# Moving the second block's first inputs into the second gate stage, and five modulation slots to the end of the recurrent mixer

## The reference

```
x = layer_norm(ALPHA * x + 0.5 * swiglu(x, ...), g, b)
y = mixer(x); x = layer_norm(ALPHA * x + y, g, b)
x = layer_norm(ALPHA * x + 0.5 * swiglu(x, ...), g, b)
x = x + sigmoid(x @ ple_wg + ple_bg) * (p @ ple_wp)
```

```
h  = x  * (1 + sc1)  + sh1      # tokens
hc = xc * (1 + csc1) + csh1     # context, from the input
q, k, v = split(h @ w_in), split(hc @ w_in)
```

## Time and profile before

| | |
|---|---|
| median of 3 runs | 2394.52 us (2393.4 to 2398.42) |
| profiled execution | 2394.99 us, its span 2393.7 |
| mean granted TensorE clock | 0.975 of full |
| PE busy | 94% of the span |
| DVE, ACT, POOL busy | 53%, 45%, 2% |
| DMA | 353.6 MB, mean 148 GB/s |

### The profile page before, as it was taken

One profiled execution on the slowest core, in us unless ns is written; L12 is line 12 of the kernel. 1 busy time (PEld: TensorE's weight loads), 2 busy tenths in 40 slices (PEclk: granted clock), 3 DMA queues, 4 the chain that ended last, 5 costly groups with the idle time before them and its releaser, 6 DMA issues.

```text
span 2393.7 us, 39354 instructions
## 1 busy us (share of the span) xinstructions
PE 2254.1 (94%) x17046; PEld 2022.7 (85%) x17046; DVE 1269.7 (53%) x1954; ACT 1077.3 (45%) x1713; POOL 54.3 (2%) x100
## 2 busy tenths in 40 slices
PE   6999989999999999989996989999999999998998
PEld 5999869998999799879995766888888886567997
DVE  3445566556555666365556326764443663455665
ACT  3444455445444554354445526552332451354544
POOL 0000100000000000000000000000000000000000
PEclk9999999999999999989998999999999999999999
DMA  8454525545554544245545121022223433203451
GB/s 315 177 193 176 224 106 218 198 165 218 188 193 168 209 187 165 106 179 195 190 159 194 71 71 53 1 106 89 88 88 119 155 131 129 100 13 138 186 194 54
DMA packets 51628, 353.60 MB, mean 148 GB/s; under 512 B 8064, under 2 KB 8448, under 8 KB 8832
## 3 DMA queue, kind: packets, MB, share of 16 engines
q1 hardware_dynamic: 47520, 346.05, 38.5%
q10 hardware_dynamic: 864, 4.63, 0.5%
q0 software_dynamic: 3072, 0.40, 0.1%
HBM read 349.61 MB, written 1.05 MB: 146 GB/s over the span
## 4 chain that ended last, share of the span: by engine, by line
PE 86%; DVE 7%; ACT 3%; DMA 1%; issue 1%; SPq 0%; POOL 0%; ACTq 0%; DVEq 0%
PE ps L784 13%; PE ps L785 13%; PE ps L786 13%; PE ps L2490 5%; PE ps L920 5%; PE ps L2491 5%; PE ps L2492 5%; PE ps L390 3%; PE ps L391 2%; PE ps L392 2%; PE ps L2220 2%; PE ps L2221 2%; PE ps L2222 2%; PE ps L1455 1%; PE ps L973 1%; PE ps L986 1%
## 5 line engine op out<-in xcount | busy, mean ns | idle before, releaser
L365 DVE TENSOR_TENSOR wl<-ring,wh 128x1024 fp32r<-128x1024 f32 x406 | 477.6, 1221 | 269.1 <-ACT wh L360 268.9
L784 PE MATMUL ps<-xs,wh 128*128 128x256 f32 x1760 | 503.8, 286 | 27.0 <-DVE wl L365 14.1
L785 PE MATMUL ps<-xs,wl 128*128 128x256 f32 x1760 | 502.1, 285 | 0.0
L786 PE MATMUL ps<-xs,wh 128*128 128x256 f32 x1760 | 501.9, 285 | 0.0
L360 ACT ACTIVATE wh<-ring 128x1024 fp32r<-128x1024 f32 x406 | 405.0, 1049 | 167.0 <-PE ps L786 127.1
L784 PEld LDWEIGHTS ps<-xs,wh 128*128 128x128 f32 x1760 | 342.1, 194 | 31.0 <-issue 21.0
L785 PEld LDWEIGHTS ps<-xs,wl 128*128 128x128 f32 x1760 | 342.3, 194 | 0.0
L786 PEld LDWEIGHTS ps<-xs,wh 128*128 128x128 f32 x1760 | 342.1, 194 | 0.0
L784 PE MATMUL ps<-hh,wh 128*128 128x256 f32 x880 | 249.2, 283 | 0.7 <-DVE hl L886 0.7
L785 PE MATMUL ps<-hh,wl 128*128 128x256 f32 x880 | 249.1, 283 | 0.0
L786 PE MATMUL ps<-hl,wh 128*128 128x256 f32 x880 | 249.1, 283 | 0.0
(11 more groups left out here) (441 smaller groups left out, 4016.7 us busy)
## 6 DMA issues: line engine op xcount, KB each, us to landing
ring<-wstream SPq DMA_DIRECT2D x329, 1024.0 KB, 4.9
ada_rows<-ada_stage POOLq DMA_DIRECT2D x96, 4.0 KB, 4.1
CN<-consts ACTq DMA_DIRECT2D x1, 1136.0 KB, 15.7
X<-xin ACTq DMA_DIRECT2D x1, 1024.0 KB, 10.6
X<-cin ACTq DMA_DIRECT2D x1, 1024.0 KB, 9.2
out<-X SPq DMA_DIRECT2D x1, 1024.0 KB, 3.9
PT__65<-pin ACTq DMA_DIRECT2D x1, 512.0 KB, 18.9
ab_w<-wab ACTq DMA_DIRECT2D x1, 512.0 KB, 3.5
```

What stands on the lines that cost most here:

```text
L365: dve.tensor_tensor(lo, tile_of(i), hi.bitcast(F32), ALU.subtract).then_inc(low_part, 1)
L784: pe.matmul(out, wh[:, w, c, :], x_hi, start=start, stop=False, skip_group_check=True)
L785: pe.matmul(out, wl[:, w, c, :], x_hi, start=False, stop=False, skip_group_check=True)
L786: return pe.matmul(out, wh[:, w, c, :], x_lo, start=False, stop=True, skip_group_check=True)
```

## The change

- Five of the modulation slots move from the second gate stage to the end of the recurrent mixer, between the second and the third `c_out` slot in load order; PE multiplies them right after the mean squares. The last z tile moves ahead of the last output products, and all silus come before the norm.
- `pe_adaln` and `dve_adaln` move into the second gate stage, behind its first two tiles. The context is loaded at the end of the recurrent mixer, and `ple_pp` moves to other memory.
- In the second gate stage ACT modulates the context, DVE each finished chunk of x, and both split the results and the first even slot, between the gate tiles. The scaling by ALPHA comes later.
- In the first gate stage the first four weight tiles of `ffn1_1` are split between the gate tiles, and the input's high parts follow chunk by chunk.
- `X` is no longer written ahead of the gate: its sum takes the norm's offset directly.

```
-            + [("ple_g_0", 1), ("ada", 1)] * 4 + [("ada", 1), ("ffn1_1", 33), ("ada", 3), ("c_g", 1)]
+            + [("ple_g_0", 1), ("ada", 1)] * 2 + [("ple_g_0", 2), ("ada", 3), ("ffn1_1", 33), ("ada", 3), ("c_g", 1)]
...
-            + [("c_out", 4), ("ada", 3), ("ffn2_1", 33), ("ple_p_1", 1)] + [("ple_g_1", 1), ("ada", 1)] * 4
-            + [("ada", 1), ("l0_in", 9), ("rpb", 2), ("l0_out", 4), ("l0_ffn", 40),
+            + [("c_out", 2), ("ada", 5), ("c_out", 2), ("ada", 3), ("ffn2_1", 33), ("ple_p_1", 1), ("ple_g_1", 4)]
+            + [("l0_in", 9), ("rpb", 2), ("l0_out", 4), ("l0_ffn", 40),
...  pe_ple
-            pe_ada(8)
+            pe_ada(8) if i == 0 else pe_adaln()
             for t in range(2, 8):
                 pe.wait_ge(*((ple_proj, 4 * i + t + 1) if t < 4 else (ple_gate, 8 * i + t - 3)))
                 pe_tile(t0 + t, PLE_BANK[t % 4])
-                if t % 2:
+                if i == 0 and t in (3, 5):
                     pe_ada(8)
-            pe_ada(8)
+            if i == 0:
+                pe_ada(16)
...  act_ple
-                if t + 4 < 8:
+                if i == 0 or t + 4 < 8:
                     act_high(t0 + t + 4)
+                if i == 0 and t in (3, 5, 6):
+                    act_ada(128 + {3: 8, 5: 16, 6: 24}[t])
+                if i == 1:
+                    if t in (2, 3, 4, 5):
+                        act_context(2 * t - 4)
+                        act_context(2 * t - 3)
+                    if t == 4:
+                        act_slot_high(0)
+                    for q in {5: (0, 1), 6: (2,), 7: (3,)}.get(t, ()):
+                        act_even_high(q)
+            if i == 0:
+                for q in range(4):
+                    c = slice(2 * q, 2 * q + 2)
+                    act.wait_ge(x_ple, 2 * q + 2)
+                    act.activation(xs[:, c, 0, :], X[:, 0, c, :], ACT.Copy).then_inc(x_high, 1)
...  dve_ple
-            dve_x(f"ffn2_{i}")
-            dve.wait_ge(*x_normed(f"ffn2_{i}"))
+            name = f"ffn2_{i}"
+            dve.wait_ge(z_gained, 8 * LNS.index(name) + 8)
+            if i == 1:
+                dve_adaln()
             for t in range(8):
-                if t + 4 < 8:
+                if i == 0 or t + 4 < 8:
                     dve_low(t0 + t + 4)
...
-                dve.scalar_tensor_tensor(X[:, 0, t, :], ple_th[:, t, :], 0.5, X[:, 0, t, :], ALU.mult,
+                dve.scalar_tensor_tensor(X[:, 0, t, :], Z[:, 0, t, :], pcol(LN_GB[name][1], t), ple_th[:, t, :], ALU.add,
                                          ALU.add).then_inc(x_ple, 1)
+                if i == 1:
+                    if t >= 3:
+                        for c in {3: (0, 1), 4: (2, 3), 5: (4, 5), 6: (6,), 7: (7,)}[t]:
+                            dve_modulate(c)
+                    if t == 4:
+                        dve_slot_low(0)
+                    for q in {5: (0,), 6: (1, 2), 7: (3,)}.get(t, ()):
+                        dve_even_low(q)
+            if i == 0:
+                dve_xlow("ffn1_1", X[:, 0])
...  pe_mixer_c
             outputs(2, 2)
+            tile(31)
             outputs(3, 7)
...
             pe.wait_ge(*c_o_a.at("ln1"))
-            pe_ada(8)
+            pe_ada(48)
...  act_mixer_c
             norm_o(2, 0)
             norm_o(3, 1)
-            act_high(t0 + 35)
-            act_ada(320)
-            act.wait_ge(*c_o_v.at("z0"))
+            act_ada(328)
             for k in range(4):
-                if k == 1:
-                    act.activation(c_z[:, 6:8, :], c_z[:, 6:8, :], ACT.Silu).then_inc(*c_o_a("z67"))
                 act.wait_ge(*c_o_v.at(f"z{k}"))
                 act.activation(xs[:, 2 * k:2 * k + 2, 0, :], c_o[:, 2 * k:2 * k + 2, :], ACT.Copy).then_inc(x_high, 1)
+                act_ada(336 + 8 * k)
```

More of the change, by code:

```diff
@@ L180, in _plan @@
     first, last, both = TILE0["c_k"], TILE0["c_out"] + 8, TILE0["l0"]
+    gate = TILE0["ple_g_1"]
     for i in range(len(TILES)):
-        BUF.append((i - first) % 4 if first <= i < last else (i - both) % 4 if both <= i < both + 7 * NPAIR else i % NB)
+        BUF.append((2, 3, 4, 5, 2, 3, 0, 1)[i - gate] if gate <= i < gate + 8 else (i - first) % 4 if first <= i < last else (i - both) % 4 if both <= i < both + 7 * NPAIR else i % NB)
         PREV.append(max((j for j in range(i) if BUF[j] == BUF[i]), default=None))
@@ L197 @@
 LN_COLS = ["l0_1", "l0_2", "l1_1"]
-X_MADE = ["ffn1_0", "ffn2_0", "ffn1_1", "ffn2_1", "l1_2"]
+X_MADE = ["ffn1_0", "ffn1_1", "l1_2"]
 LN_AB = {"ffn2_0": ("ab", 2), "ffn2_1": ("c", 10)}
@@ L829, in act_ffn @@
                 act.wait_ge(gate_up_done, NT * f)
-            if src is not None:
+            else:
                 act_xhigh(src)
@@ L868, in dve_ffn @@
             i0 = TILE0[name]
-            if src is not None:
+            if f == 0:
                 dve_xlow(name, src)
@@ L1306, in dve_add_branch @@
             dve.scalar_tensor_tensor(z, row(t % 4), coef, z, ALU.mult, ALU.add).then_inc(z_done, 1)
-        ple_pp, ple_th = (put(n, [8, T], over=(b, 8192)) for n, b in (("ple_pp", "X"), ("ple_th", "Z")))
+        ple_th = put("ple_th", [8, T], over=("Z", 8192))
+        ple_pp = put("ple_pp", [8, T], over=("free", 512))
         ple_hb = put("ple_hb", [2, 8], over=("free", 0))
@@ L1330, in act_ple_proj @@
                 act.wait_ge(*raw_tile(f"ple_p_{i}", 2 * k + 1))
-                act.activation(flat(ple_pp, k), ps[:, (6, 7, 0, 1)[k], :], ACT.Copy).then_inc(ple_proj, 1)
+                act.activation(flat(ple_pp, k), ps[:, (6, 7, 0, 1)[k], :], ACT.Copy, scale=0.5).then_inc(ple_proj, 1)
         def pe_ple(i):
@@ L1436, in build_program @@
         c_o_p = Steps(sem("c_out_tensor"), [f"o{c}" for c in range(4)] + [f"var{c}" for c in range(4)])
-        c_o_a = Steps(sem("c_out_scalar"), [f"sq{c}" for c in range(4)] + [x for c in range(4) for x in (f"ln{c}", f"rn{c}")]
-                      + ["z67"])
+        c_o_a = Steps(sem("c_out_scalar"), [f"sq{c}" for c in range(4)] + [x for c in range(4) for x in (f"ln{c}", f"rn{c}")])
         c_o_v = Steps(sem("c_out_vector"), [f"r{c}" for c in range(4)] + [f"z{n}" for n in range(4)])
@@ L1860, in z_tile @@
                 act.wait_ge(*tile_done(t0 + 24 + t))
-                act.activation(c_z[:, t, :], row(t % 2), ACT.Silu if t < 6 else ACT.Copy).then_inc(c_z_a, 1)
+                act.activation(c_z[:, t, :], row(t % 2), ACT.Silu).then_inc(c_z_a, 1)
             z_tile(0)
@@ L2360, in square @@
                 act.activation(e_sq[:, u % 2, :], ps[:, E_BANK[u], :], ACT.Square).then_inc(e_sq_a, 1)
[L2361 to L2365, removed]
             act_slot_high(1)
@@ L2379, in act_even_mixer @@
             act_slot_high(4)
+            act.wait_ge(x_ple, 16)
+            act_scale("even", slice(0, 2))
             for t in range(4):
@@ L2413, in dve_even_mixer @@
         def dve_even_mixer():
[L2414 to L2428, removed]
             dve_slot_low(1)
@@ L3006, in act_program @@
             act_layer_norm("ffn2_0", ahead=tiles("ple_g_0"))
-            act_ple(0, "ffn2_0")
-            act.wait_ge(x_ple, 8)
-            act_ffn(2, "ffn1_1", X[:, 0], copies=168)
+            act_ple(0)
+            act_ffn(2, "ffn1_1", X[:, 0], ahead=4, copies=168)
             act_layer_norm("ffn1_1", 192, ahead=tiles("c_k"))
             act_mixer_c()
-            act_layer_norm("c", 344, ahead=tiles("ffn2_1"))
+            act.dma_start(X[:, 1, :, :], cin).then_inc(in_ctx, 16)
+            act_layer_norm("c", 384, ahead=tiles("ffn2_1"))
             act_ffn(3, "ffn2_1", None, ahead=2)
             act_layer_norm("ffn2_1", ahead=tiles("ple_g_1"))
[L3015 to L3018, removed]
+            act_ple(1)
             act_even_mixer()
@@ L3049, in dve_program @@
             dve_ple(0)
-            dve_ffn(2, "ffn1_1", X[:, 0], half)
+            dve_ffn(2, "ffn1_1", X[:, 0], half, ahead=4)
             dve_norm_to_parts("ffn1_1", tiles("c_k"))
```

58 lines of the change are left out of this document (37 added, 21 removed).

## The result

The changed kernel took 2371.06 us (median of 4 runs, 2367.02 to 2374.37) beside 2393.96 us for the kernel before on the same chip: ratio 0.9912, 95% interval 0.9896 to 0.9927, so about 22.9 us faster. The profiled execution took 2374.37 us, at a span of 2373.1. In a second series on another occasion it took 2366.55 us beside 2391.44 (ratio 0.9902, 0.9887 to 0.9917), 24.9 us faster. Forecast were 2368.0 us and 26.5 us of gain.

The account below looks back on a forecast made before the run. TensorE, busy 94% of the span, was taken as the bound, so gains lie in its pauses, double work or low clock. -26.0 - 4.5 + 4.0 = -26.5 from 2394.99 gave 2368.5, forecast 2368 us; range 2361 to 2379.

Parts of the forecast that it names:

- Part C: Second gate stage into the first even tile: tile ends at 1297.4 instead of 1323.4, gain 26.0 us (20 to 28).
- about half a microsecond: Second gate stage: tanh 5 and 6 on ACT run this late, and no gate tile waits for them.
- the longer queue: Second gate stage: DVE's queue outlasts ACT's, its last low part ending at 1295.4 after ACT's last high part.
- hidden work is not hidden: Rival, 16%: second gate stage's modulation and splitting still follow the last gate tile; gain 16.5 instead of 26, 2377.5 us.
- The steps taken to cost nothing: Later ALPHA scaling in the second gate stage costs nothing; context load at the mixer's end costs nothing (0 to 1 us).
- Part B: Recurrent mixer's end: six modulation slots wait for ring loads, `c_out` starts 5.8 us later; cost 4 us (0 to 8).
- the 1.7 forecast: Within `c_out`: the low clock loses 2.4 us instead of 4.1, so 1.7 us of the later start is taken back.
- the tail is cheap: Rival, 14%: at the mixer's end loads land faster or PE's own tail is shorter; cost 0, 2364 us.
- Part A: First gate stage into `ffn1_1`: early weight splits shorten PE's pause and keep the clock up; gain 4.5 us (1 to 7.5).
- perhaps 0.3 later, since ACT first waits for the slot: First gate stage: the last tanh is done at 592.8 or 0.3 later; `ffn1_1` starts at 596.9, 2.7 us less.
- The second term: Start of `ffn1_1`: a pause of 2.7 us leaves the clock alone, saving the 1.8 us lost at half clock before.
- the one row behind the pause at 802.25: Kernel before: a PE pause of 2.67 us left the clock at 1.00, so low clock was not expected after similar pauses.

Follow-up runs that it names:

- two early tiles: Changed kernel, but only two of the four first `ffn1_1` weight tiles are split early in the first gate stage: 2362.21 us, ratio to before 0.9874.
- both edits: Changed kernel with two early `ffn1_1` tiles instead of four and three of the five tail slots inside the mixer's z tiles: 2356.99 us, ratio 0.9859.
- small loads: Changed kernel, but three of the five modulation slots at the mixer's end load only 256 of 2048 columns (output wrong): 2359.05 us, ratio 0.9870.

## Why the prediction was right, and where not

**Part C, the second gate stage, was sized right: 25.9 us measured (25.5 in the second execution), 26.0 forecast.** `pe_adaln` takes 1.42 us (12 matmuls at 1275.54; 1.4 forecast) in the gate stage. The pauses for the second and fourth quarter of the input are 0.73 and 1.84 us ("about 1 and 2"), and the first even tile is done 8.6 us behind the last gate tile (8.5). This is ScalarE's timeline there:

```profile
1292.12 0.46 ACT L1357 ACTIVATE ple_th<-ps,ple_hb 128x256 f32<-128x256 f32 x1
1292.91 1.06 ACT L1426 ACTIVATE e_xh<-H 128x1024 fp32r<-128x1024 f32 x1 [0.33 <-DVE H L1419]
1294.36 0.48 ACT L1357 ACTIVATE ple_th<-ps,ple_hb 128x256 f32<-128x256 f32 x1 [0.39 <-PE ps L393]
1298.92 1.06 ACT L1426 ACTIVATE e_xh<-H 128x1024 fp32r<-128x1024 f32 x1 [4.09 <-DVE H L1419]
...
1303.00 0.60 ACT L2411 ACTIVATE e_sq<-ps 128x512 f32<-128x512 f32 x1 [1.22 <-PE ps L2274]
```

ScalarE stood idle for 0.39 us ahead of the last tanh, waiting for its tile, so the added work fits; the two tanh before it had no idle time ahead of them, 0.3 and 0.7 us late by the step of 2.87 us ("about half a microsecond"). The last high part waits 4.09 us for the vector engine, which was named as the longer queue. The clock was 1.00 there, as forecast. That is not certain, though: in the second execution it fell behind the 1.82 us pause, at a cost of about 2 us (last section); in the five other executions with these splits between the tiles it stayed at 1.00. The runs bear the mechanism out: put the splits behind the tiles, and 9.0 us come back; the rival "hidden work is not hidden" had priced that at 9.5. The steps taken to cost nothing cost nothing: the rest of the kernel is 1070.1 us for 1070.2 of before, and the early context load landed 4.7 us after its issue at 1042.87 (9.2 in before) with nothing waiting for it.

**Part B, the mixer's tail, was right in mechanism: 4.0 forecast, 5.0 in the first execution, 4.2 by the means of all.** Slots 3 to 5 were to land at 1020.7, 1023.3 and 1025.9; they were taken at 1020.61, 1024.84 and 1027.25, and `c_out` started at 1029.11 instead of 1027.8. The later start is partly given back, since the clock comes back sooner within `c_out`: 7.1 us late at the start, 4.78 late at `ffn2_1` (1064.88 for 1060.10), so 2.3 for the 1.7 forecast. The rival "the tail is cheap" fell: no execution with all its slots and full loads had a tail of before's length (the shortest was 47.0).

**Part A, the first gate stage, was wrong in size: 4.5 forecast, 0.4 to 0.6 measured.** The step that failed is "perhaps 0.3 later, since ACT first waits for the slot". ScalarE waited for three loads (3.90, 1.04 and 1.97 us), the last tanh came 1.7 us later than in before, and the input's high parts, which stand behind the last early cast in its order, came with it. The product began at 598.74 and not at 596.9. The second term went with the first: the pause was 3.37 us and not 2.7, and the clock fell to 0.50 as in before, so the 1.8 us of clock were not gained. That term had a weak premise besides: it took the one row behind the pause at 802.25 as what such a pause does, and in eight of the ten traces the clock fell to half behind that very pause (last section). The run with two early tiles shows that the idea was sound and its amount too large: 5.9 us in the stage, more than the 4.5 forecast.

**The sum.** By stages it is -25.9 + 4.2 - 0.6 = -22.3, measured 22.9 and 24.9, forecast 26.5. Between forecast and stages the miss is the first part's 3.9 us; the rest agrees within half a microsecond. The timed medians test this less sharply: the same kernel's two lie 4.5 us apart (2371.06 and 2366.55), so that the total came within 3.1 us of the forecast says little by itself. Two slips in the recorded working are small: the half clock ahead of 603.5 lasts 3.9 us from 599.61 and not 3.7, and 1.07 x 2 is 2.1, not 1.9 (the slots took 1.94).

## What to carry to other kernels

Work that is moved ahead into an in-order queue brings its waits along: before an engine with slack is given a weight split early, look when the load that it reads lands, and what the engine serves behind it. Filling an engine's pause with work that needs loads of its own pays only if these loads are there in time; the same slots cost 4.2 us when their loads came one behind another and, with short loads, were worth 4.5. A chain of splits is hidden by interleaving it with the products ahead of it (9 us here); the larger part of the gain (16.8 us) was there with the inputs early and the slots gone, before any interleaving.

## What the runs showed of the hardware

**The granted clock also falls without a pause.** At the mixer's end the changed kernel's two executions ran the same instructions. Windows of 4 us (us, PE busy, clock, DMA share, GB/s), first and second execution:

```profile
984.00:988.00 4.00, 4.00 (x36) 1.00 0.72 262
988.00:992.00 4.00, 4.00 (x24) 0.63 0.65 266
992.00:996.00 4.00, 4.00 (x21) 0.52 0.01 2
996.00:1000.00 4.00, 4.00 (x32) 0.91 0.00 0
```

```profile
984.00:988.00 4.00, 4.00 (x35) 1.00 0.97 410
988.00:992.00 4.00, 4.00 (x36) 1.00 0.03 6
992.00:996.00 4.00, 4.00 (x35) 1.00 0.00 0
996.00:1000.00 4.00, 4.00 (x37) 1.00 0.00 0
```

TensorE is busy throughout in both, and ahead of the fall it had done some 6 us of products with 64 to 128 columns (L1579, L1590, L1593, 16 each, from 983.78 on). In one execution the clock went to 1.2 GHz behind them and in the other it stayed at 2.4. By the windows from 988 to 1004 it lost 5.1 us there ((0.37 + 0.48 + 0.09 + 0.34) x 4, the last from 1000 to 1004), of the 7.15 us between the two executions. Another 1.7 us stand at 856 to 860, again with TensorE busy throughout (0.58 in the first execution, 1.00 in the second). The trace of before has the fall as well (0.65, 0.92, 0.93, 0.50 and 0.71 from 988 to 1008), so it does not come with the change. What decides it was not tried.

**A pause of 2.67 us mostly did not leave the clock alone, and once a pause of 1.82 us did not either.** In before the clock stayed (1.00 in 802 to 804), and in the kernel with both edits. In the other eight traces the same pause (2.66 or 2.67 us) was followed by 0.50 for some 3 us, at once in both executions of the changed kernel and in the one with small loads, within the first microsecond in the other five. At the end of the second gate stage, for which the prediction took the row of before as a rule, the clock stayed behind pauses of 0.73 and 1.84 us in the first execution of the changed kernel and fell behind the same pauses (0.74 and 1.82) in the second. First the pause of 2.67 us in the changed kernel, then the second execution's even tile:

```profile
802.00:804.00 2.00, 2.00 (x11) 0.50 0.96 406
```

```profile
1292.00:1294.00 2.00, 2.00 (x7) 0.70 0.00 0
1294.00:1296.00 2.00, 2.00 (x6) 0.50 0.00 0
```

With 0.95 from 1296 to 1298 that is 1.7 us lost ((0.30 + 0.50 + 0.05) x 2), most of the 2.0 us by which this execution's last two stages are longer (0.4 and 1.6).

**Loads of one queue landed later the more stood ahead.** At the mixer's end SyncE issues six ring loads of 1 MB in the changed kernel:

```profile
1015.68 7.25 SPq L3109 DMA_DIRECT2D ring<-wstream  x6
```

```profile
DMA to landing us min/median/max: 4.9/11.6/14.8
```

```profile
1020.00:1024.00 4.00, 1.94 (x16) 0.50 1.03 421
```

From issue to landing it is 4.9 us at the least, 11.6 in the median and 14.8 at the most, while the DMA engines move 421 GB/s; three such loads had taken 4.8 to 7.3 us.

**A small transfer may be slowed by a large one.** In the kernel before with the early context load, the modulation rows (4 KB each) were there with a pause of 7.16 us for 9.69, though no work ahead of them had changed. From issue to landing the slowest of the transfers from 1280 us on took 5.5 us there and 7.9 in before. That the context's 1 MB stood beside them on the DMA engines in before is the likely cause; it was only argued.
